# Attention stage of a two-layer hybrid decoder step reordered: decode steps, gate rows and block compression mixed into its preparation

## What is computed

```
def nsa_mixer(p, pos0, win_prefix, prm, past):            # q 4 heads, k/v 2 heads of 64
    qn = rms_norm(q, g[0]);  q_rot = rope(qn, pos)
    slc_new, win_new = keys rms_norm'ed and roped, values plain
    # compressed branch: blocks of 32 tokens, stride 16, flattened, a two-layer MLP (w1, gelu, w2)
    hid = pe @ w1 + sum_r sub[:, r:r + n_cmp] @ w1[:, r*16:(r+1)*16]
    k_cmp, v_cmp = rms_norm(gelu(hid) @ w2 [k]), gelu(hid) @ w2 [v]
    p_cmp = softmax(qn . k_cmp * SCALE);  o_cmp = p_cmp @ v_cmp
    # selected branch: the 16 blocks of 64 tokens with the largest p_cmp (decode: from paged cache)
    o_slc = softmax(q_rot . k_selected) @ v_selected
    # window branch: the last 512 tokens
    o_win = softmax(q_rot . k_window) @ v_window
    o = g0 * o_cmp + g1 * o_slc + g2 * o_win;  return o * silu(z)
```

## Time and profile before

| | us |
|---|---|
| median of 3 runs | 1631.5 (1629.0 to 1635.43) |
| profiled execution, its own time | 1647.69 |
| its span | 1646.0 |
| first layer's attention, from the end of T3's tiles to the first output matmul | 499.0 to 758.3 |
| the same in the second layer | 1308.5 to 1569.7 |

### The profile page before, as it was taken

One profiled execution on the slowest core, in us unless ns is written; L12 is line 12 of the kernel. 1 busy time (PEld: TensorE's weight loads), 2 busy tenths in 40 slices (PEclk: granted clock), 3 DMA queues, 4 the chain that ended last, 5 costly groups with the idle time before them and its releaser, 6 DMA issues.

```text
span 1646.0 us, 28542 instructions
## 1 busy us (share of the span) xinstructions
PE 1441.9 (88%) x9880; PEld 1033.4 (63%) x9880; DVE 804.2 (49%) x2008; ACT 393.5 (24%) x765; POOL 170.3 (10%) x310
## 2 busy tenths in 40 slices
PE   5998999898998986769999899998989899776795
PEld 3764777888854773444458377788877448634542
DVE  1445547656453285652125465575463425756410
ACT  4230102112111243441332110131110113425300
POOL 0000000000000233440000000000000003344200
PEclk9997989978799996789999779999687999777898
DMA  7132422410031344466242233122100404363621
GB/s 297 66 105 75 145 66 77 156 52 2 1 131 64 119 117 142 138 203 267 75 158 75 81 103 131 52 85 96 52 2 1 189 6 148 107 201 108 238 84 64
DMA packets 92930, 175.94 MB, mean 107 GB/s; under 512 B 14081, under 2 KB 79794, under 8 KB 86898
## 3 DMA queue, kind: packets, MB, share of 16 engines
q1 hardware_dynamic: 80066, 124.58, 22.7%
q0 software_dynamic: 12720, 49.54, 8.7%
HBM read 161.27 MB, written 21.12 MB: 111 GB/s over the span
## 4 chain that ended last, share of the span: by engine, by line
PE 71%; DVE 10%; issue 10%; DMA 3%; POOLq 3%; ACT 2%; POOL 1%; SPq 0%; DVEq 0%; ACTq 0%
PE bank L562 15%; PE bank L599 14%; PE bank L1164 8%; PE bank L2640 3%; POOLq L386 2%; PE bank L495 2%; PE bank L1298 2%; PE bank L795 2%; PE bank L1190 2%; PE bank L1286 1%; DMA stream<-in_slcV 1%; PE bank L1275 1%; DVE area L1641 1%; PE bank L565 1%; PE bank L803 1%
## 5 line engine op out<-in xcount | busy, mean ns | idle before, releaser
L562 PE MATMUL bank<-stream,hT 128*128 128x512 f32 (+3 forms) x768 | 263.6, 501 | 14.6 <-ACT area L575 14.1
L599 PE MATMUL bank<-hT,stream 128*128 128x272 f32 x960 | 229.3, 401 | 5.1 <-DVE area L1530 5.1
L562 PEld LDWEIGHTS bank<-stream,hT 128*128 128x128 f32 x768 | 147.3, 195 | 115.5 <-issue 101.6
L599 PEld LDWEIGHTS bank<-hT,stream 128*128 128x128 f32 x960 | 185.4, 194 | 44.5 <-DVE area L1530 5.3
L1164 PE MATMUL bank<-stream,prm 128*128 128x256 f32 x512 | 126.1, 409 | 0.4 <-DVE YT L1511 0.4
L2640 PE MATMUL bank<-stream,YT 128*128 128x512 f32 x256 | 112.6, 601 | 4.8 <-DVE YT L2546 4.8
L1164 PEld LDWEIGHTS bank<-stream,prm 128*128 128x128 f32 x512 | 104.7, 207 | 18.1 <-issue 1.7
L2640 PEld LDWEIGHTS bank<-stream,YT 128*128 128x128 f32 x256 | 48.9, 192 | 66.1 <-issue 60.8
L2299 ACT ACTIVATE area<-area 128x256 f32<-128x256 f32 (+3 forms) x96 | 52.2, 544 | 140.1 <-DVE area L2596 138.5
L392 POOL DMA_DIRECT2D stream<-in_slcV x128 | 71.3, 558 | 85.1 <-PE bank L2037 23.4
L392 POOL DMA_DIRECT2D stream<-in_slcK x128 | 68.5, 535 | 108.5 <-PE bank L2181 35.0
(11 more groups left out here) (609 smaller groups left out, 2339.6 us busy)
## 6 DMA issues: line engine op xcount, KB each, us to landing
stream<-in_cmpL SPq DMA_DIRECT2D x256, 128.0 KB, 2.3
stream<-in_win_ SPq DMA_DIRECT2D x12, 2048.0 KB, 8.6
stream<-in_slcK SPq DMA_DIRECT2D x128, 64.0 KB, 2.2
stream<-in_slcK POOLq DMA_DIRECT2D x128, 64.0 KB, 2.4
stream<-in_slcV SPq DMA_DIRECT2D x128, 64.0 KB, 2.2
stream<-in_slcV POOLq DMA_DIRECT2D x128, 64.0 KB, 2.5
stream<-in_wout SPq DMA_DIRECT2D x4, 2048.0 KB, 9.7
out_winpast<-in_winraw POOLq DMA_DIRECT2D x2, 4064.0 KB, 25.8
```

The source lines that it names most:

```text
L562: last = nc.tensor.matmul(ps[:, 0:w], hT[:, k, tok(i)], ws[:, k, :], start=(k == 0), stop=(k == KT - 1))
L599: last = nc.tensor.matmul(ps[:, 0:HALF], ws[:, k, 128 * f:128 * f + 128], hT[:, k, HALF * s:HALF * s + HALF], start=(k == 0), stop=(k == K ...
```

## The change

1. **T3 early.** ACT copies T3's first tile in `act_r`, the others as the first thing of `act_n`; the gelu of the cache blocks moves to an idle place in RWKV; DVE clears PN's tail before `dve_r_norm`; the shift state is stored under a semaphore of its own. The RWKV transposes (`pe_r_end`) stand after T3's fourth tile.
2. **Preparation mixed.** Head transposes, key norm and block transposes stand between T5's tiles, and the decode scores `ds` 0 to 3, the compressed decode scores, the block choice and the prompt's compressed scores between the gate rows of F3. The features FT have a place of their own (they lay in hT, which F3 reads).
3. **Packed compression.** `pe_block_hidden` multiplies over 128 rows (two token positions) with `w1p`, 32 passes in place of 64. `w1f` and its slot are gone; the pair after slcK 1 is skipped in the slot order so that winK takes F3's pair.
4. **Decode softmax by quarters.** ACT copies `ds` out of PSUM, DVE masks it in SBUF and takes the maximum of each quarter; the exp is in parts at units 6, 7 and 8; only the output is scaled.
5. **Loop order.** Scores of unit u + 2 stand before the transposes of u; values of a pair one unit later; DVE runs step, mask of u + 2, scaling of u + 1 (it ran scaling, step, mask); the mask is written in place in PSUM and the bank is freed by ACT's exp. The decode steps come earlier: window and memory scores at 3 and 4, turns from 8, values from 12.
6. **Copies and pages.** ACT's decode step precedes the unit's copy. Page numbers are loaded early and kept in registers. x is read back in two parts.

The core of the diff:

```diff
@@ items, sync_stream, pool_pages, pool_r
-            items += [("w", l, n) for n in ("T2", "T3", "T4", "T5")] + [("w1f", l), ("w", l, "F3")]
+            items += [("w", l, n) for n in ("T2", "T3", "T4", "T5", "F3")]
+            if it[0::2] == ("slcK", 2):
+                at_slot += n
+                elif it == ("w", l, "T4"):
+                    for c in range(3):
+                        kept[c] = read_pages(sp, c, 0)
+                if it[0::2] in (("slcK", 0), ("slcV", 2)):
+                    kept[3] = read_pages(sp, 3, 0)
+                elif it[0::2] == ("slcK", 3):
+                    kept[0] = read_pages(sp, 0, 0)
+            pool.wait_ge(ptab_in, at("ptab"))
+            for c in range(3):
+                pool_kept[c] = read_pages(pool, c, 1)
...
@@ act_r, dve_r
+            act.wait_ge(shift_stored[l], at("so", l))
+            act.wait_ge(pe_done, at("full", "dbn", l))
+            act.wait_ge(dve_done, at("ntails", l))
+            act_take_heads(act, l, 0)
             act.wait_ge(dve_done, at("v20", l))
...
             dve_r_dec(dve, l)
+            dve(nc.vector.memset(PN[:, 4, 0:1166], 0.0).then_inc(dve_done, 1), "ntails", l)
             dve_r_norm(dve, l)
...
@@ pe_n
-            pe_project_tm(pe, l, "T3")
-            pe_r_end(pe, l)
+            for i in range(TILES):
+                if i == 4:
+                    pe_r_end(pe, l)
+                pe_project_tile(pe, l, "T3", i)
...
+            for i in range(TILES):
+                pe_project_tile(pe, l, "T5", i)
+                pe_head_turn(pe, l, i)
+                if i == 1:
+                    pe_block_rows(pe, l)
+                elif i == 2:
+                    pe_key_norm(pe, l, 0)
+            pe_block_hidden(pe, l)
             pe_project_rows(pe, l, "F3", 0)
+            pe_decode_scores(pe, l, 0)
+            pe_decode_cmp(pe, l)
+            pe_cmp_kv(pe, l, "p")
             pe_project_rows(pe, l, "F3", 1)
+            pe_decode_scores(pe, l, 1)
+            pe_key_norm(pe, l, 1)
+            pe_gates(pe, l)
+            for i in range(TILES):
+                pe_mem_head_turn(pe, l, i)
             pe_project_rows(pe, l, "F3", 2)
+            pe_decode_weights(pe, l)
+            pe_decode_scores(pe, l, 2)
+            pe_block_scores(pe, l)
+            pe_unit_s(pe, l, 0)
+            pe_unit_s(pe, l, 1)
+            pe_project_rows(pe, l, "F3", 3, (4, 5))
+            pe_decode_blocks(pe, l)
+            pe_decode_scores(pe, l, 3, 7)
...
@@ pe_block_hidden
-                for s in range(16):
-                    last = nc.tensor.matmul(ps[:, 64 * c:64 * c + 64], wf[:, c, s, :], kv[:, c, :, :, s], start=(s == 0), stop=(s == 15))
+                for j in range(8):
+                    last = nc.tensor.matmul(ps[:, 64 * c:64 * c + 64], w1p[:, c, j, :], KVT[:, c, :, :, j], start=(j == 0), stop=(j == 7))
...
@@ steps and loop
+        TSTEP = (8, 9, 10, 11, 15, 16)
+        VSTEP = (12, 13, 14, 17, 18, 20)
             for u in range(len(UNITS)):
-                pe_unit_t(pe, l, u)
-                pe_decode_step(pe, l, u)
                 if u + 2 < len(UNITS):
                     pe_unit_s(pe, l, u + 2)
-                if u % 2:
-                    pe_unit_v(pe, l, u)
+                pe_unit_t(pe, l, u)
+                if u and u % 2 == 0:
+                    pe_unit_v(pe, l, u - 1)
+                pe_decode_step(pe, l, u)
...
             for u in range(len(UNITS)):
+                act_decode_step(act, l, u)
                 act_unit_t(act, l, u)
                 if u + 2 < len(UNITS):
                     act_unit_e(act, l, u + 2)
-                act_decode_step(act, l, u)
...
@@ dve_decode_mask, dve_prompt
+            dve.wait_ge(act_done, at("DS", l, c))
+            dve(nc.vector.tensor_tensor(sb3, sb3, off, ALU.add).then_inc(dve_done, 1))
+            dve(nc.vector.reduce_max(DMX[:, c:c + 1], sb, axis=AX.X).then_inc(dve_done, 1))
...
             for u in range(len(UNITS)):
+                dve_decode_step(dve, l, u)
+                if u + 2 < len(UNITS):
+                    dve_unit_m(dve, l, u + 2)
                 if u + 1 < len(UNITS):
                     dve_unit_p(dve, l, u + 1)
                 if u and u % 6 == 0:
                     dve_unit_o(dve, l, u // 6 - 1)
-                dve_decode_step(dve, l, u)
-                if u + 2 < len(UNITS):
-                    dve_unit_m(dve, l, u + 2)
```

More of the change, by code:

```diff
@@ L158 @@
 }
-INS = ["const", "prm", "x", "memx", "wmem", "win_", "wout", "w1f", "ptab", "cmpL", "slcK", "slcV", "winK", "memK",
+INS = ["const", "prm", "x", "memx", "wmem", "win_", "wout", "ptab", "cmpL", "slcK", "slcV", "winK", "memK",
        "winV", "memV", "winraw",
@@ L347, in slot, with read_pages @@
             return stream[:, s * SLOT:(s + 2) * SLOT]
+        def read_pages(L, c, hf):
+            return [L.eng.value_load(ptab[0:1, w:w + 1], min_val=0, max_val=NPOOL - 1) for w in key_pages(c, hf)]
         def sync_stream(sp):
+            kept = {}
             for it in items:
@@ L359, in sync_stream @@
                         which = [it[2] * NPAGE + g for g in range(NPAGE)]
+                        page = [sp.eng.value_load(ptab[0:1, w:w + 1], min_val=0, max_val=NPOOL - 1) for w in which]
                     else:
-                        which = key_pages(it[2], 0)
-                    page = [sp.eng.value_load(ptab[0:1, w:w + 1], min_val=0, max_val=NPOOL - 1) for w in which]
+                        page = kept[it[2]]
+                elif it == ("w", l, "T4"):
+                    for c in range(3):
+                        kept[c] = read_pages(sp, c, 0)
                 for old in before[it]:
@@ L1951, in pe_n, with pe_head_turn, pe_mem_head_turn @@
             phase_end(pe, "N", l)
+        def pe_head_turn(pe, l, i):
+            n = rows(i)
+            pe.wait_ge(dve_done, at("rope", l, i))
+            ps = pe.open("fa", l, i)
+            for a in range(4):
+                src = PN[0:n, i, 128 * a:128 * a + 128] if a < 2 else QR[0:n, i, 128 * a - 256:128 * a - 128]
+                last = nc.tensor.transpose(ps[:, n * a:n * a + n], src, idn[0:n, 0:n])
+            pe.full(last.then_inc(pe_done, 1), "fa", l, i)
+        def pe_mem_head_turn(pe, l, i):
+            n = rows(i)
+            pe.wait_ge(dve_done, at("mqn", l))
+            ps = pe.open("fb", l, i)
+            for a, o in enumerate((1024, 1152, 256, 384)):
+                last = nc.tensor.transpose(ps[:, n * a:n * a + n], PN[0:n, i, o:o + 128], idn[0:n, 0:n])
+            pe.full(last.then_inc(pe_done, 1), "fb", l, i)
         def pe_block_bias(pe, l):
@@ L2154, in pe_prompt @@
                         o = 128 * i + 64 * g + 32 * h
-                        last = nc.tensor.matmul(ps[:, o:o + 32], FT[half(h), FQN + g, tok(i)], KC[half(h), 1024:1056], start=True, stop=True)
+                        last = nc.tensor.matmul(ps[:, o:o + 32], FT[FQN + g][half(h), tok(i)], KC[half(h), 1024:1056], start=True, stop=True)
                 if h == 0:
@@ new lines, in dve_decode_mask, with act_decode_scores @@
+        def dve_decode_mask(dve, l, c):
+            dve.wait_ge(act_done, at("DS", l, c))
+            sb, off = SB[:, 512 * c:512 * c + 512], bc(BI[:, 8 * c:8 * c + 8], 2, SLC_BLOCK)
+            sb3 = sb.rearrange("p (n j) -> p n j", j=SLC_BLOCK)
+            dve(nc.vector.tensor_tensor(sb3, sb3, off, ALU.add).then_inc(dve_done, 1))
+            dve(nc.vector.reduce_max(DMX[:, c:c + 1], sb, axis=AX.X).then_inc(dve_done, 1))
+        def act_decode_scores(act, l, c):
+            act.wait_ge(pe_done, at("full", "ds", l, c))
+            act(nc.scalar.copy(SB[:, 512 * c:512 * c + 512], bank("ds", l, c)[:, :]).then_inc(act_done, 1), "DS", l, c)
+            act.free("ds", l, c)
@@ L2563, in dve_prompt @@
             dve_unit_m(dve, l, 0)
+            dve_unit_m(dve, l, 1)
             dve.wait_ge(act_done, at("PCe", l))
```

455 lines of the change are left out of this document (247 added, 208 removed).

## The result

The changed kernel took 1535.9 us (median of 4, 1529.3 to 1541.8) against 1633.5 before; the ratio is 0.941, 95% interval 0.935 to 0.947. On another chip it was 1532.1 (median of 6), ratio 0.935 (0.929 to 0.940). The forecast was 1538, in a range of 1510 to 1570. Its profiled execution took 1540.6, its span is 1538.9, 107.1 less than before.

The account below looks back on a forecast made before the run. TensorE, busy 88% of the span, was taken as the bound, through idle time, low clock and work. 15 us before the loop plus 32 in it make 47 a layer, 94 in all: 1631.5 − 94 = 1538 us, range 1510 to 1570.

Parts of the forecast that it names:

- The likeliest case: Whole kernel: 15 us before the loop plus 32 in it, 47 a layer, 94 in all, to 1538 us; chance 0.57.
- T3 early: Before the loop, at T4: TensorE's 7.06 us wait goes and T4's first tile takes 7.13 for 9.03; 9.0 us a layer.
- Packed compression: Block compression before the loop: half of 64 passes, half of 7.29 us, so 3.6 us a layer won.
- Preparation mixed: Before the loop: waits of 5.58 and 4.44 go, 4.0 of cold work goes, 1.7 wait comes; −12.3 us a layer.
- Loop: Attention loop: units sum to 90.7 us, plus 1 of page wait, taken as 92; −32 us a layer.
- The wait for the fourth value quarter: In the loop: its pages land 18 to 19.5 us after the slot frees; a wait of 1 us, between 0 and 4.
- Nothing outside attention: Code outside attention: nothing changes but x's return in two parts, counted as nothing.
- Tables: ScalarE: four more table loads a layer at 1.28 us each; by the skill page's 2.66, 8 us longer in time.
- the account by stalls: TensorE's idle stretches before and in the loop, 43.7 us a layer, each paid twice through slow-clock work behind it.
- the price by unit: Loop: each unit costs the larger of TensorE's and VectorE's work, as the new order gives a unit's lead; sum 90.7 us.
- that of the transfers: Rival: earlier consumers wait on the same DMAs in attention, 16 of the 47 us given back, 1570 us; chance 0.18.
- low clock through the loop: Rival: small waits tied to VectorE keep TensorE at 1.2 GHz in the loop; +24 us, 1655; chance 0.03.

## Why the prediction was right

The likeliest case held: 47 us a layer were forecast and attention is shorter by 49.1 and 51.1. The part ahead of the loop fell short by 1.5 and 2.0, and the loop gave 3.5 and 6.0 more, so that errors cancelled in part. Each step can be set beside what it measured.

- **T3 early.** 9.0 forecast; from T3's fourth tile to the end of T4's first it is 19.24 before and 10.16 after, 9.08. Undone it costs 9.3 and 7.6.
- **Packed compression.** 3.6 forecast; from its start to the next gate part 7.11 before, 3.86 after: 3.25. But twice the passes cost only 0.7 and 2.0 before the loop, since the 1.79 us of wait for the gelu take a share. The forecast had both, 3.6 won and 1.7 paid, 1.9 net; alone the packing is worth no more than that.
- **Preparation mixed.** 5.58 and 4.44 are gone, and 1.79 came for the 1.7 forecast. The step that failed is what the move does to the clock: 2.2 and 2.9 us in the fourth gate part, behind 3.7 us of narrow passes. That is most of why the loop starts 13.5 and 13.0 us earlier and not 15.
- **Loop.** 92 forecast, 88.5 and 88.2 measured. By the starts of the transposes: units 0 to 3 took 14.5 for 13.2, units 4 to 7 13.8 for 13.5, 8 to 11 13.1 for 13, 12 to 17 24.5 for 25, from 18 on 22.5 for 26. The larger of TensorE's and VectorE's work in each unit was a good price. In the last stretch TensorE's pieces come to 19.8 for the 22.2 priced, and its waits to 2.7 for 3.8. The clock is 0.94 and 0.92 where 0.93 or more was named. The price of units 8 to 11 held, 13.1 for 13, but not its reason: all parts of the exp at one step cost 1.4 and 1.2, and the stall of 4.19 goes with the order alone.
- **The wait for the fourth value quarter.** 1 us forecast; the page costs about 0.7 in the first layer and nothing in the second (the expectation for late page numbers misread the 1.65 and 1.00 as a page's). The size was right and the reasoning too small: keeping the numbers was taken as a start saved once (4 us in the expectation), and is 9 us of every 18.3, worth 15 to 18 us a layer.
- **Nothing outside attention.** The 6.9 us there are within scatter, so neither a gain nor a loss is shown. The forecast named only x's return; the copies, the gelu and the clear that moved into RWKV lie there too.
- **Tables.** The wait behind the chain of three loads measured 1.79 and 1.61, as priced at 1.28 a load.

What was wrong is the account by stalls, in the first part of the prediction: 43.7 us of idle stretches, 26.6 of them in the loop, each with its own cure. In the loop they are not additive. Two chains held it, each for itself: the order of scores, mask, scaling and transposes, and the pages, 18.3 us for each quarter on POOL. Cure the first alone, and the loop is 123.3 and 125.9 us, as before (124.0 and 126.2). Leave the first and cure the second, with every other part in place: 131.2 and 129.0, though some of these waits are that mixture's own. With both: 88.5 and 88.2. The forecast came out because the price by unit assumed both at once. Of the rivals, that of the transfers is what happens as soon as the page numbers are loaded late; low clock through the loop did not come (0.94), but TensorE's order undone shows what it costs: a clock of 0.81 and 17.9 us of longer pieces among the 38.5 given back.

The cause of 100 us in attention is thus shown for the orders, the page numbers and T3; packed compression, the exp by parts and the positions of the values are shown to be small alone. The mixing of the preparation, which also takes the decode scores out of the loop, was not undone; its two waits of 5.58 and 4.44 are read from the trace. With late page numbers the fourth value product starts 76.9 us after the loop's start and not 107.9, so a good part of the page chain was shortened by these earlier steps, and how much by which stays open. So does what the mask in place in PSUM and the positions of the turns are worth.

## What to carry to other kernels

When a loop shows several long waits on different releasers, ask how often each resource can deliver, and compare the rates: a stall that is cured can move to the next chain, and a part tried alone can show nothing and yet be needed. In a pipeline over engines the order on one engine is only good with its partner on the other: put what releases the other engine (scores for the next mask) ahead of what waits for it. Register loads ahead of DMA issues belong in the time in which the engine waits for a slot.

## What the runs showed of the hardware

**A stretch of narrow passes lowered the clock.** In the first layer TensorE was busy without a gap, for 3.4 us with passes of 64x32, when the granted clock went from 1.00 to 0.50, 2.4 to 1.2 GHz. In the second layer it fell 4.7 us after their start, in the gap of 0.55 behind them. With about 1.9 us of them, 512-wide passes, and the rest of them it stayed at 1.00 in both layers, gap and all. The low level lasted 4.4 and 5.7 us into the wide passes of the gate part. The Trainium skill, page "TensorE: Matmul & The Clock Gate", section "Part 1: The HAM clock gate", ties the clock to activity; the trace agrees only in part, since in the first layer it fell while the view shows TensorE busy throughout.

**Loading 16 page numbers into registers takes POOL 8.7 to 8.8 us**, about 0.55 each, nearly what the 16 issues take (9.3). The loads have no rows of their own; it is the pause ahead of the issues, and with kept numbers it is gone.

**Untouched code varies by up to 20 us.** Windows from the first output matmul to the end of T3's fourth tile of the next layer, first of the changed kernel, then with the narrow passes split, then with the value products late:

```profile
704.23:1250.83 546.60, 516.50 (x3315) 381.87 (x3316) 263.85 (x595) 110.15 (x186) 10.75 (x20) 0.89 0.24 83
```

```profile
703.14:1242.56 539.42, 508.52 (x3315) 374.15 (x3315) 263.73 (x595) 110.17 (x186) 10.73 (x20) 0.91 0.25 84
```

```profile
706.18:1262.56 556.38, 526.91 (x3315) 391.10 (x3315) 263.71 (x595) 110.16 (x186) 10.73 (x20) 0.87 0.26 89
```

The same 3315 matmuls are busy for 508 to 527 us at a clock of 0.91 to 0.87, while VectorE's and ScalarE's times agree within 0.2. The lowest of the other kernels with this code, both orders undone, took 536.3 us there, with TensorE busy for 505.6. Effects of a few us must be read in the window that they are in; five rounds of whole times don't show them.
